# Float32 products between float16 ones: where the decay and a products, the scans and the weight splits of an RWKV-7 time mixer stand

## The chip, the cores and the metric

The kernel runs on one core of a Trainium2 chip. The metric is device time in microseconds (us) of one execution, the median of the runs shown. TensorE has two clock levels, 1.2 and 2.4 GHz; the profile gives the granted clock as a share of full speed (0.50 and 1.00).

## The reference, cut to what matters

Two layers of a streaming encoder over 528 positions (16 learned ones and 512) of 1024 channels. Each layer is a half-step SwiGLU FFN, a token mixer, another half-step FFN, each between RMSNorms. Layer 0's mixer is RWKV-7 with 16 heads of 64, layer 1's is attention in a window. The change touches RWKV-7 alone, ahead of its recurrence:

```python
xx = jnp.pad(h, ((0, 0), (1, 0), (0, 0)))[:, :-1] - h
xm = h[:, :, None, :] + xx[:, :, None, :] * mix          # r, k, v, w, a, g
rkv = jnp.einsum('blmc,mcd->blmd', xm[:, :, :3], w_rkv)
w_log = -jax.nn.softplus(-(w0 + jnp.tanh(xw @ w1) @ w2)) - 0.5
decay = jnp.exp(-jnp.exp(w_log))
a = jax.nn.sigmoid(a0 + (xa @ a1) @ a2)
g = jax.nn.sigmoid(xg @ g1) @ g2
kk = (k * k_k).reshape(B, L, H, N)
kk = kk / jnp.maximum(jnp.sqrt(jnp.sum(kk * kk, axis=-1, keepdims=True)), 1e-12)
k = k * (1 + (a - 1) * k_a)
```

Here w1 and a1 are 1024 x 64, w2 and a2 64 x 1024, g1 1024 x 160 and g2 160 x 1024.

## The kernel before, in words

Channels lie on partitions (8 tiles of 128), positions along the free axis. A large product in float32 quality is made of three float16 ones: weights and activations are each split into a high part and a rest, and high x high, high x rest and rest x high are summed in PSUM (`products`, line 287). A weight block comes by DMA into one of two halves of `stage`; ScalarE writes its high part (`split_hi`, line 256), VectorE its rest (`split_lo`, line 262). Every engine works through a program of its own in fixed order, with semaphores between them; the order is written out by hand in functions named after stage and engine.

The stages of RWKV-7 before the recurrence, in TensorE's order:

- **K**, then **V**: 8 tiles each (4 weight blocks `j` times 2 halves `s` of the positions); a tile is two groups ("halves") of 24 matmuls, one for each 128 output channels. A tile's two PSUM banks are copied out by VectorE (`evict`); three pairs of banks take turns (0 to 5), banks 6 and 7 are free for other use. During V ScalarE, VectorE and GpSimd make the mixtures for w and a: ScalarE scales the shifted input (`wa_prev`, line 942), VectorE adds (`wa_sum`, line 946), ScalarE makes the float16 high part (`wa_high`, line 951), GpSimd the rest (`wa_rest`, line 955), in four blocks `j`, each followed by one weight split.
- **The LoRA stage** (`lora_pe`, `lora_act`, `lora_dve`): first the products with w1 and a1 ("l products", `l_at`), into banks 6 and 7; tanh of the w part (`t_w`) on ScalarE, a copy of the a part (`t_a`) on VectorE. Then the gate's products with g1, four groups of 24 matmuls (`g_at`): two with 128 and two with 32 output channels. Meanwhile the mixtures for g and then for r are made; g's rests are VectorE's (line 955), and in the middle of them stands the split of R's second weight block, `r_jobs[1]`. Then the 16 products with w2 (decay, `w0` to `w7`) and a2 (`a0` to `a7`), line 1238: float32, 64 rows, two matmuls of 264 columns, four instructions each as the profile counts them. Each has two banks out of a ring of four pairs. ScalarE takes a sigmoid of each (line 1272), and VectorE a scan along time over each decay (line 1303).
- **R**: 8 tiles like V's. Between its halves stand the sums of squares over heads for kk (`sum_heads`, line 303, float32, 16 output rows; halves 1 to 4, two each) and the spreads of the inverse norms back to channels (`spread_heads`, line 311, float32, 16 rows in; halves 7 to 14, one each), all in banks 6 and 7. ScalarE makes the squares (line 1344), the root (line 1348) and the factors `f` (line 1353), VectorE the reciprocal (line 1383), and kk, k and b (`rates`, lines 1362 to 1368).
- **core**: the recurrence in chunks of 64, then the epilogue, which reads the gate and g2.

The semaphores of small steps are counters with names: `Steps.count(name)` is the place of the name in a list given once, and a wait for it waits until the counter has that value. It means "this step is done" only if steps are done in the order of the list. For `lo_act` the list is sg, sg2, tanh, w0 to w7, a0 to a7, where `sg` and `sg2` are the gate's two sigmoids (lines 1264 and 1266); ScalarE issues tanh (line 1256) first, then sg and sg2.

The activations' spill to DRAM (`s_spill`) frees the buffer `h` during these stages: it holds `sgate`, w2 and a2, `t_w`, `t_a` and r's scratch `tm_r`.

Of the kernel before, what the change touches and what calls it, by code (L numbers as in the profile page):

```python
# [22 lines left out]
ALU = mybir.AluOpType  # L23
# [74 lines left out]
def build(nc, xT, vecs, consts, w_gu, w_down, w_rkv, w_l1, w_g1, w_w2, w_a2, w_g2, w_out, w_q, w_k, w_v, b_v,  # L98
          w_o, rel_table, rel_hot, flip_rows, out):
    with ExitStack() as ctx:  # L100
# [742 lines left out]
        spreads = hflat[0:HEADS, 3104:3104 + D]  # L843
# [11 lines left out]
        def rwkv(T, T_out, ffn_before):  # L855
# [11 lines left out]
            lo_act = Steps(sem("lora_act"), ["sg", "sg2", "tanh"] + [f"{q}{k}" for q in "wa" for k in range(KT)])  # L867
# [11 lines left out]
            tm_r = hflat[:, 3104:4160].rearrange("p (s t) -> p s t", s=2)  # L879
# [201 lines left out]
            more = split_more[:, :]  # L1081
            dq = more[:, 0:2 * L].rearrange("p (u t) -> p u t", u=2)
            df = more[:, 2 * L:4 * L].rearrange("p (u t) -> p u t", u=2)
            norms = more[0:HEADS, 4 * L:5 * L]
# [3 lines left out]
            d_dve = Steps(sem("kk_dve"), ["spread", "max", "inv"] + [f"{q}{k}" for k in each for q in ("kk", "k", "b")])  # L1088
# [120 lines left out]
            seq = [(q, k) for q in "wa" for k in each]  # L1209
            rate_bank = [2 * ((g_at + 1) % 3), 6, 2 * ((g_at + 2) % 3), 2 * (g_at % 3)]  # L1210

            def lora_pe(e):
                e.wait_ge(w_lo, l_job.n + 1)
                e.wait_ge(wa_lo, 2 * KT)
                for s, q in enumerate("wa"):
# [5 lines left out]
                open_step(e, g_at, g_job)  # L1221
                for s, (c0, c1) in enumerate([(0, P), (P, 160)]):
# [5 lines left out]
                last.then_inc(done, 1)  # L1228
                e.wait_ge(s_w2, 32)
                e.wait_ge(lo_act.sem, lo_act.count("tanh"))  # L1230
                e.wait_ge(freed, l_at + 1)
                for z, (q, k) in enumerate(seq):
                    if z == 2:
                        e.wait_ge(freed, g_at + 1)
                    if z >= 4:
                        e.wait_ge(lo_act.sem, lo_act.count("%s%d" % seq[z - 4]))
                    for b, (a, m) in enumerate(ALL):
                        last = e.matmul(psum[:, rate_bank[z % 4] + b, 0:m],  # L1238
                                        (w2_sb if q == "w" else a2_sb)[:, k * P:(k + 1) * P],
                                        (t_w if q == "w" else t_a)[:, a:a + m], start=True, stop=True)  # L1240
                    last.then_inc(lo_pe.sem, lo_pe.step(f"{q}{k}"))

            def lora_act(e):
# [24 lines left out]
                e.wait_ge(padded.sem, padded.count("a"))  # L1268
                for z, (q, k) in enumerate(seq):
                    e.wait_ge(lo_pe.sem, lo_pe.count(f"{q}{k}"))  # L1270
                    dst = (c_all if q == "w" else a_all)[:, k, PAD:LP]
                    e.activation(halves(dst, n), psum[:, rate_bank[z % 4]:rate_bank[z % 4] + 2, 0:n],
                                 ACT.Sigmoid, bias=v("w0" if q == "w" else "a0", k)).then_inc(
                                     lo_act.sem, lo_act.step(f"{q}{k}"))

            def lora_dve(e):
                for k in range(4):
                    g_sum(e, k)
                for k in each:
                    g_rest(e, k)  # L1280
                    if k == 3:
                        split_lo(e, r_jobs[1])
# [17 lines left out]
                e.wait_ge(s_mask, 2)  # L1300
                for k in each:
                    e.wait_ge(lo_act.sem, lo_act.count(f"w{k}"))
                    e.tensor_tensor_scan(c_all[:, k], mask, c_all[:, k], 0.0, ALU.mult, ALU.add).then_inc(c_scan, 1)

            def gate_weights(e):

                e.wait_ge(lo_pe.sem, lo_pe.count(f"a{KT - 1}"))
                e.dma_start(g2_sb[:, 0], w_g2[0:P, :]).then_inc(s_g2, 16)
# [3 lines left out]
            def r_pe(e):  # L1312
                def sums(k0):
                    if k0 == 0:
                        e.wait_ge(lo_act.sem, lo_act.count("a5"))
                    for k in (k0, k0 + 1):
                        e.wait_ge(d_act.sem, d_act.count(f"sq{k}"))
                        sum_heads(e, 6, k, dq[:, k % 2]).then_inc(d_pe.sem, d_pe.step(f"sum{k}"))

                def inverses(k):  # L1320
                    if k == 0:
                        e.wait_ge(d_dve.sem, d_dve.count("inv"))
                    else:
                        e.wait_ge(d_dve.sem, d_dve.count(f"kk{k - 1}"))
                    spread_heads(e, 6, k, norms).then_inc(d_pe.sem, d_pe.step(f"inv{k}"))

                def after_tile(q):
                    if 1 <= q <= 4:
                        sums(2 * (q - 1))
                    elif 7 <= q <= 14:  # L1330
                        inverses(q - 7)

                for q, (j, s) in enumerate(in_order):
                    if q < 3:
                        e.wait_ge(lo_act.sem, lo_act.count(("a4", "a6", "a7")[q]))
                    tiles(e, r_at[j, s], r_jobs[j], x16, s,
                          (lambda k: e.wait_ge(r_lo, k + 1)) if q == 0 else None, None, lambda: after_tile(2 * q))
                    after_tile(2 * q + 1)

            def r_act(e):  # L1340
                for k in each:
                    if k >= 2:
                        e.wait_ge(d_pe.sem, d_pe.count(f"sum{k - 2}"))
                    e.activation(dq[:, k % 2], k_all[:, k, PAD:LP], ACT.Square, scale=v("k_k", k)).then_inc(
                        d_act.sem, d_act.step(f"sq{k}"))
                split_hi(e, r_jobs[2])
                e.wait_ge(d_pe.sem, d_pe.count(f"sum{KT - 1}"))
                e.activation(halves(norms, n), psum[0:HEADS, 6:8, 0:n], ACT.Sqrt).then_inc(
                    d_act.sem, d_act.step("root"))
                for k in each:  # L1350
                    if k >= 2:
                        e.wait_ge(d_dve.sem, d_dve.count(f"k{k - 2}"))
# [1326 lines left out]
```

## Time and profile before

| | us |
|---|---|
| median of 3 runs | 2321.61 |
| lowest and highest | 2320.35, 2323.71 |
| profiled execution | 2321.75 |
| its span | 2320.0 |
| TensorE busy in the span | 2228.7 (96%) |
| VectorE, ScalarE, GpSimd busy | 1075.0, 797.8, 500.7 |

The span is what the profiler's records cover; times of the trace count from its start. A row of the windows gives for a stretch how long each engine was busy, with the number of instructions, and TensorE's granted clock. A row of the instructions in order of time gives start, duration, engine, line, operation, operands and count, and in brackets how long the engine was idle before it and for whom. Matmul ends are modelled and overlap the next start; starts are better to count from.

### The profile page before, as it was taken

To read this page: it belongs to the slowest core of one execution; us is meant where nothing else is said; L and a number is where in the kernel's file an instruction comes from. 1 tells how busy PE (TensorE), PEld (TensorE's weight loads), DVE (VectorE), ACT (ScalarE), POOL (GpSimd) and SP (SyncE) were. 2 spreads that over 40 slices of the span, in tenths; PEclk is the share of its full clock that TensorE was granted. 3 is DMA by queue.
4 is the path that set the end of the run, shared out by engine and by line. 5 is a ranking of instruction groups with operands and counts; after the bars stand their busy time and mean duration, and the time that the engine had idled before them with its cause. 6 is when DMAs were issued, how large, how long until landed. Compare 5 with 4: busy or idle time off the path is not lost.

```text
span 2320.0 us, 50849 instructions
## 1 busy us (share of the span) xinstructions
PE 2228.7 (96%) x22812; PEld 1892.4 (82%) x22812; DVE 1075.0 (46%) x1455; ACT 797.8 (34%) x1356; POOL 500.7 (22%) x629
## 2 busy tenths in 40 slices
PE   7999999989899989899999999999999999999997
PEld 6888887877699965788888888888887668888886
DVE  5433326763566654553342273333274536533323
ACT  4333313664233331343332253333132434433320
POOL 2111114410132300531111241110153106211103
PEclk9999999997999995999999999999999779999998
DMA  4323311320000010323233123233214011232311
GB/s 157 128 97 118 125 62 55 122 73 12 2 4 4 4 41 21 142 96 110 92 119 116 41 89 113 92 113 117 80 55 118 1 37 70 100 105 101 141 51 37
DMA packets 28954, 183.42 MB, mean 79 GB/s; under 512 B 3217, under 2 KB 8145, under 8 KB 9793
## 3 DMA queue, kind: packets, MB, share of 16 engines
q1 hardware_dynamic: 27888, 178.79, 21.8%
q8 instruction: 180, 2.95, 0.5%
q0 software_dynamic: 848, 1.37, 0.3%
q14 instruction: 38, 0.30, 0.0%
HBM read 174.31 MB, written 4.30 MB: 77 GB/s over the span
## 4 chain that ended last, share of the span: by engine, by line
PE 87%; DVE 6%; POOL 3%; ACT 2%; issue 1%; DMA 0%; SPq 0%; POOLq 0%; ACTq 0%; DVEq 0%
PE psum L287 69%; PE psum L1561 5%; POOL h L347 1%; PE psum L1552 1%; PE psum L2338 1%; PE psum L2337 1%; PE psum L1894 1%; PE psum L1238 1%; PE psum L362 1%; PE psum L2324 1%; PE psum L311 1%; POOL x L398 1%; PE psum L1585 1%; PE psum L1896 1%; DVE split L262 1%
## 5 line engine op out<-in xcount | busy, mean ns | idle before, releaser
L287 PE MATMUL psum<-x,split 128*128 128x256 f16 (+1 forms) x5568 | 640.1, 277 | 10.5 <-POOL x L398 6.7
L287 PEld LDWEIGHTS psum<-x,split 128*128 128x128 f16 x5568 | 545.6, 98 | 102.1 <-issue 16.0
L287 PE MATMUL psum<-x,split_more 128*128 128x256 f16 (+1 forms) x2496 | 288.5, 277 | 1.5 <-DVE x L2436 1.5
L695 POOL TENSOR_TENSOR arena<-arena 128x256 f16<-128x256 f32 (+1 forms) x176 | 120.2, 683 | 771.3 <-ACT arena L544 771.3
L287 PE MATMUL psum<-x,arena 128*128 128x256 f16 (+2 forms) x2448 | 280.9, 276 | 0.3 <-POOL x L934 0.2
L287 PEld LDWEIGHTS psum<-x,split_more 128*128 128x128 f16 x2496 | 246.0, 99 | 38.5 <-issue 1.9
L287 PEld LDWEIGHTS psum<-x,arena 128*128 128x128 f16 (+1 forms) x2448 | 240.5, 98 | 35.0 <-POOL x L934 0.9
L262 DVE SCALAR_TENSOR_TENSOR split<-stage,split 128x2048 f16<-128x2048 f32 (+1 forms) x77 | 190.5, 2475 | 164.8 <-ACT split L256 164.8
L287 PE MATMUL psum<-arena,split 128*128 128x256 f16 (+1 forms) x2304 | 261.6, 276 | 0.0
L287 PEld LDWEIGHTS psum<-arena,split 128*128 128x128 f16 x2304 | 226.2, 98 | 33.3 <-issue 0.3
L622 DVE SCALAR_TENSOR_TENSOR arena<-psum,arena 128x256 f32<-128x256 f32 (+1 forms) x176 | 75.5, 429 | 320.8 <-ACT arena L538 316.3
L538 ACT ACTIVATE arena<-psum 128x256 f32<-128x256 f32 (+1 forms) x176 | 68.3, 388 | 384.3 <-PE psum L287 384.2
L256 ACT ACTIVATE split<-stage 128x2048 f16<-128x2048 f32 (+1 forms) x77 | 156.1, 2028 | 31.5 <-PE psum L287 29.7
L438 ACT ACTIVATE arena<-arena 128x272 f32<-128x272 f32 (+1 forms) x96 | 38.9, 418 | 360.0 <-DVE arena L425 336.9
L425 DVE TENSOR_SCALAR arena<-psum 128x272 f32<-128x272 f32 (+1 forms) x80 | 33.3, 428 | 249.6 <-PE psum L287 249.6
L287 PE MATMUL psum<-arena,split_more 128*128 128x256 f16 (+3 forms) x1248 | 144.1, 277 | 3.1 <-DVE arena L955 3.0
L287 PEld LDWEIGHTS psum<-arena,split_more 128*128 128x128 f16 (+1 forms) x1248 | 122.3, 98 | 23.0 <-DVE arena L955 4.3
L544 ACT ACTIVATE arena<-arena 128x256 f16<-128x256 f32 (+1 forms) x176 | 74.0, 421 | 185.9 <-DVE arena L627 185.9
L287 PE MATMUL psum<-arena 128*128 128x256 f16 (+2 forms) x1200 | 136.8, 275 | 0.0
L449 POOL TENSOR_TENSOR arena<-arena 128x272 f32<-128x272 f32 (+1 forms) x84 | 65.5, 780 | 324.7 <-ACT arena L438 321.5
L287 PEld LDWEIGHTS psum<-arena 128*128 128x128 f16 (+1 forms) x1200 | 117.8, 98 | 16.9 <-POOL arena L955 0.3
L262 DVE SCALAR_TENSOR_TENSOR split_more<-stage,split_more 128x2048 f16<-128x2048 f32 (+2 forms) x36 | 88.5, 2459 | 80.3 <-ACT split_more L256 80.3
(215 smaller groups left out, 2638.7 us busy)
## 6 DMA issues: line engine op xcount, KB each, us to landing
stage<-in_w_gu SPq DMA_DIRECT2D x88, 1024.0 KB, 4.9
stage<-in_w_down SPq DMA_DIRECT2D x32, 1408.0 KB, 6.0
stage<-in_w_rkv SPq DMA_DIRECT2D x12, 1024.0 KB, 4.9
stage<-in_w_out SPq DMA_DIRECT2D x4, 1024.0 KB, 4.9
stage<-in_w_q SPq DMA_DIRECT2D x4, 1024.0 KB, 4.7
stage<-in_w_o SPq DMA_DIRECT2D x4, 1024.0 KB, 6.2
h_spill<-h SPq DMA_DIRECT2D x1, 2112.0 KB, 11.6
h<-h_spill SPq DMA_DIRECT2D x1, 2112.0 KB, 11.1
```

The lines of the kernel that those rows point to most:

```text
L256: act.activation(job.split[:, 0, 0:job.cols], stage[:, job.u, 0:job.cols], ACT.Copy, scale=W_SCALE).then_inc(w_hi, 1)
L262: dve.scalar_tensor_tensor(out=job.split[:, 1, 0:job.cols], in0=stage[:, job.u, 0:job.cols], scalar=W_SCALE, in1=job.split[:, 0, 0:job.col ...
L287: last = pe.matmul(o, wt(wp, k), xs(xp, k), start=(k == 0 and wp == 0 and xp == 0), stop=(k == tiles - 1 and wp == 1))
L311: last = e.matmul(psum[:, b0 + b, 0:m], to, rows[:, a:a + m], start=True, stop=True)
L425: ins = dve.tensor_scalar(mix_out[:, m, a:a + n], bank(i, z)[:, 0:n], 1.0 / W_SCALE, None, ALU.mult)
L438: act.activation(osq[:, q % 2, 0:n], mix_out[:, m, a:a + n], ACT.Square).then_inc(out_sq, 1)
L449: pool.tensor_tensor(ssum[:, a:a + n], ssum[:, a:a + n], osq[:, q % 2, 0:n], ALU.add).then_inc(out_add, 1)
L538: e.activation(gate_s[:, no % 2, 0:n], bank(i)[:, 0:n], ACT.Sigmoid, scale=1.0 / W_SCALE).then_inc(gate_act, 1)
L544: e.activation(hid[s][:, 0, m, 0:n], hid32[:, no % 2, 0:n], ACT.Copy).then_inc(hid_hi, 1)
L622: e.scalar_tensor_tensor(out=gate_x[:, no % 2, 0:n], in0=bank(i)[:, 0:n], scalar=1.0 / W_SCALE ** 2, in1=gate_s[:, no % 2, 0:n], op0=ALU.m ...
L695: e.tensor_tensor(hid[s][:, 1, m, 0:n], hid32[:, no % 2, 0:n], hid[s][:, 0, m, 0:n], ALU.subtract).then_inc(hid_lo, 1)
L1561: last = e.matmul(o[p0:p0 + HD, q], a[p0:p0 + HD, 4 * f + q, 0:CH], b[p0:p0 + HD, 4 * f + q, 0:CH], start=(z == 0), stop=(z == len(terms) ...
```

## The change

The sums for kk move from R's halves 1 to 4 to V's halves 4 to 11 (one each), and the squares and the root with them; the squares' scratch `dq` and `norms` move into `h`, so the first square waits for the spill. The eight decay products go in pairs behind each of the gate's four groups, with two pairs of banks in place of four; tanh is now first in the list of `lo_act`. The a products go into R: one inside its first half, one after each of halves 0 to 6, all in banks 6 and 7. The eight scans, the reciprocal and the split of `r_jobs[1]` move into R on VectorE, the split's high part into R on ScalarE. The loads of g2 now wait for the last spread too. The spreads stay behind halves 7 to 14.

```diff
-            lo_act = Steps(sem("lora_act"), ["sg", "sg2", "tanh"] + [f"{q}{k}" for q in "wa" for k in range(KT)])
+            lo_act = Steps(sem("lora_act"), ["tanh"] + [f"w{k}" for k in range(KT)] + ["sg", "sg2"] + [f"a{k}" for k in range(KT)])
...
             def v_pe(e):
-                for j, s in in_order:
+                def sums(q):
+                    k = q - 4
+                    if 0 <= k < KT:
+                        e.wait_ge(d_act.sem, d_act.count(f"sq{k}"))
+                        sum_heads(e, 6, k, dq[:, k % 2]).then_inc(d_pe.sem, d_pe.step(f"sum{k}"))
+
+                for q, (j, s) in enumerate(in_order):
                     tiles(e, v_at[j, s], v_jobs[j], xa0, s,
-                          (lambda k: e.wait_ge(v_lo, k + 1)) if j == 0 and s == 0 else None)
+                          (lambda k: e.wait_ge(v_lo, k + 1)) if q == 0 else None, None, lambda: sums(2 * q))
+                    sums(2 * q + 1)
...
                     split_hi(e, v_after[j])
+                    if j == 0:
+                        e.wait_ge(s_spill, 16)
+                    for k in range(4 * j, 4 * j + 4):
+                        if k < KT:
+                            if k >= 2:
+                                e.wait_ge(d_pe.sem, d_pe.count(f"sum{k - 2}"))
+                            e.activation(dq[:, k % 2], k_all[:, k, PAD:LP], ACT.Square, scale=v("k_k", k)).then_inc(
+                                d_act.sem, d_act.step(f"sq{k}"))
+                e.wait_ge(d_pe.sem, d_pe.count(f"sum{KT - 1}"))
+                e.activation(halves(norms, n), psum[0:HEADS, 6:8, 0:n], ACT.Sqrt).then_inc(
+                    d_act.sem, d_act.step("root"))
...
-            rate_bank = [2 * ((g_at + 1) % 3), 6, 2 * ((g_at + 2) % 3), 2 * (g_at % 3)]
+            rate_bank = [2 * ((g_at + 1) % 3), 6]
...
             def lora_pe(e):
                 e.wait_ge(w_lo, l_job.n + 1)
                 e.wait_ge(wa_lo, 2 * KT)
+                e.wait_ge(d_act.sem, d_act.count("root"))
...
-                last.then_inc(done, 1)
-                e.wait_ge(s_w2, 32)
-                e.wait_ge(lo_act.sem, lo_act.count("tanh"))
-                e.wait_ge(freed, l_at + 1)
-                for z, (q, k) in enumerate(seq):
-                    if z == 2:
-                        e.wait_ge(freed, g_at + 1)
-                    if z >= 4:
-                        e.wait_ge(lo_act.sem, lo_act.count("%s%d" % seq[z - 4]))
...
+                        for u in range(2):
+                            if k == 0:
+                                e.wait_ge(s_w2, 32)
+                                e.wait_ge(lo_act.sem, lo_act.count("tanh"))
+                                e.wait_ge(freed, l_at + 1)
+                            if k >= 2:
+                                e.wait_ge(lo_act.sem, lo_act.count(f"w{k - 2}"))
+                            rate_product(e, "w", k, rate_bank[k % 2])
+                            k += 1
...
                 for k in each:
                     g_high(e, k)
-                    if k == 3:
-                        split_hi(e, r_jobs[1])
...
+                e.wait_ge(padded.sem, padded.count("c"))
                 for k in range(0, KT, 2):
                     for u in range(2):
                         r_prev(e, k + u)
                     for u in range(2):
                         r_high(e, k + u)
+                    for u in range(2):
+                        rate(e, "w", k + u, rate_bank[u])
...
                     g_rest(e, k)
-                    if k == 3:
-                        split_lo(e, r_jobs[1])
...
                 def after_tile(q):
+                    if q < KT - 1:
+                        e.wait_ge(lo_act.sem, lo_act.count(f"a{q}"))
+                        rate_product(e, "a", q + 1, 6)
+                    elif q < 2 * KT - 1:
+                        k = q - KT + 1
+                        if k == 0:
+                            e.wait_ge(lo_act.sem, lo_act.count("a7"))
+                            e.wait_ge(d_dve.sem, d_dve.count("spread"))
+                        else:
+                            e.wait_ge(d_dve.sem, d_dve.count(f"kk{k - 1}"))
+                        spread_heads(e, 6, k, norms).then_inc(d_pe.sem, d_pe.step(f"inv{k}"))
+
+                def first_rate(e, T, s):
+                    e.wait_ge(lo_act.sem, lo_act.count("w7"))
+                    rate_product(e, "a", 0, 6)
+
+                e.wait_ge(lo_act.sem, lo_act.count("w6"))
...
             def r_act(e):
+                e.wait_ge(padded.sem, padded.count("a"))
+                rate(e, "a", 0, 6)
+                split_hi(e, r_jobs[1])
+                for k in range(1, KT):
+                    rate(e, "a", k, 6)
+                    if k == 4:
+                        split_hi(e, r_jobs[2])
+                    if k < 3:
+                        factor(e, k - 1)
+                split_hi(e, r_jobs[3])
+                for k in range(2, KT):
+                    factor(e, k)
...
                 e.memset(r_all[:, :, 0:PAD], 0.0).then_inc(padded.sem, padded.step("r"))
+                split_lo(e, r_jobs[1])
+                e.wait_ge(d_act.sem, d_act.count("root"))
+                e.tensor_scalar(norms, norms, 1e-12, None, ALU.max).then_inc(d_dve.sem, d_dve.step("max"))
+                e.wait_ge(d_dve.sem, d_dve.count("max"))
+                e.reciprocal(norms, norms).then_inc(d_dve.sem, d_dve.step("inv"))
+                evict(e, r_at[0, 0], 0, 0, r_all)
                 e.wait_ge(r_lo, KT)
...
-                evict(e, r_at[0, 0], 0, 0, r_all)
+                e.wait_ge(s_mask, 2)
+                scan(0)
+                scan(1)
                 evict(e, r_at[0, 1], 0, 1, r_all)
+                scan(2)
+                scan(3)
                 split_lo(e, r_jobs[2])
...
                 evict(e, r_at[1, 0], 1, 0, r_all)
+                for k in range(4, KT):
+                    scan(k)
                 evict(e, r_at[1, 1], 1, 1, r_all)
```

`rate_product` is the two matmuls of one product, `rate` the wait for it with its sigmoid, `scan(k)` the wait for the sigmoid `w{k}` with its scan, `factor` the factor `f{k}`; the instructions are those of before.

## Rows read from the trace of the kernel before

**Rows 1.** The page: the span, and TensorE's granted clock in 40 slices of 58 us.
```profile
span 2320.0 us, 50849 instructions
...
PEclk9999999997999995999999999999999779999998
```

**Rows 2.** Windows by stretch: engines busy (x instructions), granted clock, DMA share, GB/s.
```profile
442.80:486.30 43.50, 43.49 (x387) 37.42 (x385) 26.39 (x30) 28.75 (x41) 22.58 (x20) 1.00 0.29 99
486.30:496.80 10.50, 10.50 (x98) 10.07 (x98) 9.53 (x12) 7.40 (x12) 0.00 (x0) 1.00 0.29 101
496.80:513.00 16.20, 13.05 (x97) 9.47 (x96) 15.55 (x22) 13.79 (x22) 0.00 (x0) 0.89 0.19 66
513.00:518.10 5.10, 0.07 (x2) 0.06 (x1) 3.22 (x6) 4.75 (x7) 0.00 (x0) 0.78 0.00 0
518.10:545.00 26.90, 26.90 (x65) 20.23 (x66) 11.78 (x10) 10.41 (x15) 0.00 (x0) 0.50 0.00 1
545.00:550.00 5.00, 5.00 (x23) 3.36 (x24) 0.00 (x0) 1.95 (x3) 0.00 (x0) 0.50 0.38 131
550.00:608.20 58.20, 58.20 (x427) 42.33 (x425) 29.01 (x35) 16.96 (x19) 0.00 (x0) 1.00 0.00 1
```

**Rows 3.** TensorE's instructions in order of time, gate's groups and the first products.
```profile
500.53 0.51 PE L287 MATMUL psum<-arena,split_more 128*128 128x264 f16 x3 [2.25 <-DVE arena L955]
501.83 11.21 PE L287 MATMUL psum<-arena,split_more 128*128 128x264 f16 x81 [0.79 <-DVE arena L955]
518.07 26.90 PE L1238 MATMUL psum<-h 64*128 64x264 f32 x64 [5.03 <-issue]
```

**Rows 4.** ScalarE's instructions in order of time: sigmoid's table, sg, sg2, w0's sigmoid.
```profile
515.59 1.28 ACT L1264 ACT_TABLE_LOAD   x1
516.88 0.61 ACT L1264 ACTIVATE h<-psum 128x528 f32<-128x528 f32 x1
517.39 0.58 ACT L1266 ACTIVATE h<-psum 32x528 f32<-32x528 f32 x1
520.26 0.70 ACT L1272 ACTIVATE arena<-psum,vec 128x528 f32<-128x528 f32 x1 [2.29 <-PE psum L1238]
```

**Rows 5.** TensorE's instructions in order of time, R: sums and a spread between halves.
```profile
557.66 1.95 PE L303 MATMUL psum<-split_more,cst 128*16 128x264 f32 x8
559.55 2.79 PE L287 MATMUL psum<-x,split 128*128 128x256 f16 x24
...
577.05 1.15 PE L311 MATMUL psum<-split_more,h 16*128 16x264 f32 x4
578.14 2.95 PE L287 MATMUL psum<-x,split 128*128 128x272 f16 x24
```

**Rows 6.** VectorE's instructions in order of time: first g sums, the split, t_a, a scan.
```profile
489.17 2.80 DVE L946 SCALAR_TENSOR_TENSOR arena<-arena,omm 128x528 f32<-128x528 f32 x4
...
496.88 2.29 DVE L262 SCALAR_TENSOR_TENSOR split<-stage,split 128x2048 f16<-128x2048 f32 x1 [0.81 <-ACT split L256]
...
503.04 0.71 DVE L1287 TENSOR_SCALAR h<-psum 64x528 f32<-64x528 f32 x1
...
521.07 1.36 DVE L1303 TENSOR_TENSOR_SCAN arena<-cumsum_buf,arena 128x576 f32<-128x576 f32 x1 [3.45 <-ACT arena L1272]
```

**Rows 7.** ScalarE's instructions in order of time: a split, four scaled copies, a square.
```profile
483.79 1.90 ACT L256 ACTIVATE split<-stage 128x2048 f16<-128x2048 f32 x1
485.64 2.62 ACT L942 ACTIVATE arena<-arena,vec 128x528 f32<-128x528 f32 x4
...
564.26 0.74 ACT L1344 ACTIVATE split_more<-arena,vec 128x528 f32<-128x528 f32 x1 [0.15 <-PE psum L303]
```

**Rows 8.** Windows of 2 us, epilogue and attention.
```profile
848.00:850.00 2.00, 1.42 (x8) 0.58 (x6) 1.87 (x3) 0.64 (x1) 0.00 (x0) 1.00 0.00 0
...
1836.00:1838.00 2.00, 2.00 (x10) 1.04 (x10) 0.00 (x0) 2.00 (x11) 0.00 (x0) 0.71 0.00 0
```

**Rows 9.** TensorE's instructions in order of time, attention: start of a float32 run.
```profile
1831.94 0.43 PE L2337 MATMUL psum<-arena 128*64 128x128 f32 x2
```

More of the change, by code:

```diff
@@ L842, in build @@
         sgate = hflat[:, 0:2 * L].rearrange("p (m t) -> p m t", m=2)
-        spreads = hflat[0:HEADS, 3104:3104 + D]
+        spreads = hflat[0:HEADS, 3168:3168 + D]
         w2_sb = hflat[0:HD, 1056:2080]
@@ L1087, in rwkv @@
             d_pe = Steps(sem("kk_pe"), [f"{q}{k}" for q in ("sum", "inv") for k in each])
-            d_dve = Steps(sem("kk_dve"), ["spread", "max", "inv"] + [f"{q}{k}" for k in each for q in ("kk", "k", "b")])
+            d_dve = Steps(sem("kk_dve"), ["max", "inv", "spread"] + [f"{q}{k}" for k in each for q in ("kk", "k", "b")])
             def early(e):
@@ L1206, in v_pool, with rate_product, rate @@
                 e.memset(starts[:, :, 0:1], 0.0).then_inc(s_mask, 1)
-            seq = [(q, k) for q in "wa" for k in each]
-            rate_bank = [2 * ((g_at + 1) % 3), 6, 2 * ((g_at + 2) % 3), 2 * (g_at % 3)]
+            rate_bank = [2 * ((g_at + 1) % 3), 6]
+            def rate_product(e, q, k, b0):
+                for b, (a, m) in enumerate(ALL):
+                    last = e.matmul(psum[:, b0 + b, 0:m], (w2_sb if q == "w" else a2_sb)[:, k * P:(k + 1) * P],
+                                    (t_w if q == "w" else t_a)[:, a:a + m], start=True, stop=True)
+                last.then_inc(lo_pe.sem, lo_pe.step(f"{q}{k}"))
+            def rate(e, q, k, b0):
+                e.wait_ge(lo_pe.sem, lo_pe.count(f"{q}{k}"))
+                dst = (c_all if q == "w" else a_all)[:, k, PAD:LP]
+                e.activation(halves(dst, n), psum[:, b0:b0 + 2, 0:n], ACT.Sigmoid,
+                             bias=v("w0" if q == "w" else "a0", k)).then_inc(lo_act.sem, lo_act.step(f"{q}{k}"))
             def lora_pe(e):
@@ L1221, in lora_pe @@
                 open_step(e, g_at, g_job)
+                k = 0
                 for s, (c0, c1) in enumerate([(0, P), (P, 160)]):
@@ L1227, in lora_pe @@
                                         (lambda k: e.wait_ge(g_lo, k + 1)) if s == b == 0 else None)
-                last.then_inc(done, 1)
-                e.wait_ge(s_w2, 32)
-                e.wait_ge(lo_act.sem, lo_act.count("tanh"))
-                e.wait_ge(freed, l_at + 1)
-                for z, (q, k) in enumerate(seq):
-                    if z == 2:
-                        e.wait_ge(freed, g_at + 1)
-                    if z >= 4:
-                        e.wait_ge(lo_act.sem, lo_act.count("%s%d" % seq[z - 4]))
[L1237 to L1241, printed above, removed]
+                        if s == b == 1:
+                            last.then_inc(done, 1)
+                        for u in range(2):
[7 more added lines that the diff above has]
+                            k += 1
             def lora_act(e):
@@ L1267, in lora_act @@
                              scale=1.0 / W_SCALE).then_inc(lo_act.sem, lo_act.step("sg2"))
[L1268 to L1274, printed above, removed]
             def lora_dve(e):
@@ L1299, in lora_dve @@
                 e.memset(eps[:, 2:3], 0.0).then_inc(freed, 1)
[L1300 to L1303, printed above, removed]
             def gate_weights(e):
                 e.wait_ge(lo_pe.sem, lo_pe.count(f"a{KT - 1}"))
+                e.wait_ge(d_pe.sem, d_pe.count(f"inv{KT - 1}"))
                 e.dma_start(g2_sb[:, 0], w_g2[0:P, :]).then_inc(s_g2, 16)
@@ L1312, in r_pe @@
             def r_pe(e):
[L1313 to L1325, printed above, removed]
@@ L1338, in r_pe @@
                     after_tile(2 * q + 1)
             def r_act(e):
[L1341 to L1349, printed above, removed]
@@ L1350, in r_act @@
-                for k in each:
-                    if k >= 2:
-                        e.wait_ge(d_dve.sem, d_dve.count(f"k{k - 2}"))
-                    e.activation(df[:, k % 2], a_all[:, k, PAD:LP], ACT.Identity, bias=ka1[:, k:k + 1],
-                                 scale=v("k_a", k)).then_inc(d_act.sem, d_act.step(f"f{k}"))
-                    if k == 1:
-                        split_hi(e, r_jobs[3])
+                e.wait_ge(padded.sem, padded.count("a"))
+                rate(e, "a", 0, 6)
@@ new lines, in r_act, with factor @@
+                split_hi(e, r_jobs[1])
[8 more added lines that the diff above has]
+                    factor(e, k)
+            def factor(e, k):
+                if k >= 2:
+                    e.wait_ge(d_dve.sem, d_dve.count(f"k{k - 2}"))
+                e.activation(df[:, k % 2], a_all[:, k, PAD:LP], ACT.Identity, bias=ka1[:, k:k + 1],
+                             scale=v("k_a", k)).then_inc(d_act.sem, d_act.step(f"f{k}"))
```

27 lines of the change are left out of this document (10 added, 17 removed).

## The prediction

> **What bounds the kernel now.** I read the page first, then a table of windows over the part of the time mixer that the change touches, then the instructions of each engine there in order of time. The page shows a TensorE that is busy nearly throughout, with one slice (522 to 580 us) where the granted clock sinks to 7 tenths [rows 1]. So TensorE sets the time, and a change can gain only where TensorE waits, or where it is busy at the lower of its two clocks. The table shows both [rows 2]. V (442.8 to 486.3) and R's later part (550.0 to 608.2) are full at clock 1.00 (2.4 GHz). In the gate's four groups (496.8 to 513.0) TensorE is idle 3.2 of 16.2 us. Then it stands 5.1 us. Then the 16 decay and a products fill 26.9 us at 0.50, which is 1.2 GHz, and R's first 5.0 us are at 0.50 too. The clock fell around 516, during the 5 us of standing, and the half-row float32 products that followed did not bring it back in 26.9 us of unbroken work. R's dense float16 did within 5 us.
>
> The 5.1 us are a count and no computation. The products wait for `lo_act.count("tanh")`; in the old list `tanh` is third, behind `sg` and `sg2`, but it is issued first. A count of three is reached only when the second gate sigmoid ends: it starts at 517.39 and takes 0.58, and the first product starts at 518.07 [rows 3, 4]. The profile calls this "issue".
>
> **The change, part by part.** All positions are on the profiled execution, 2321.75 us (its span and 1.75 around it); the median of the runs shown, 2321.61, is 0.14 below.
>
> *The wait for the gate's sigmoids* goes, since `tanh` is now first in the list: 5.0 us gained (5.03 by its row [rows 3]).
>
> *Products at the full clock.* A pair of sums over heads is eight instructions of the same 264 columns in float32 and takes 1.88 us at 1.00 (557.66 to the next tile half at 559.55), and one spread is four and takes 1.09 (577.05 to 578.14) [rows 5]. I take 1.98 for each of the four pairs of decay products (0.1 for returning to float16; bounds 1.8, below the pair shown, and 2.2, two spreads) and 1.05 for each a product by itself (bounds 0.94, half a pair, and 1.1): 4 x 1.98 + 8 x 1.05 = 16.3 us for what takes 26.9. Gain 10.6.
>
> *The gate's four groups.* The l products before them show 10.5 us for four such groups [rows 2]. The groups take 16.2, so 5.7 are waits and low clock: 2.25 + 0.79 for VectorE's rests, and a fall of the clock behind them [rows 3]. VectorE sets this: from 489.17 to 503.04 it makes sums and rests, with a weight split of 2.29 in the middle (496.88) and 0.8 of waiting for that split's other half [rows 6]. The split moves into R, so the chain is 13.9 - 3.1 = 10.8 us. Where does it begin? See V, next: 497.9, so it ends at 508.7, while TensorE reaches the first group at 505.4 and would end it at 508.0. The last rest holds it until 509.05: a wait of 1.0. VectorE's copy of `t_a` (0.7) follows and the first pair begins at 509.4: 0.35 more. Gain 5.7 - 1.35 = 4.3.
>
> *The sums into V.* TensorE's part: four pairs at 1.98 leave R, eight single ones at 1.05 enter V, 0.5 lost; V then lasts 43.5 + 8.4 = 51.9 us and ends near 494.9. ScalarE's part is where a stall could come from. A square is 0.74 us, and square k waits for sum k-2, so behind block j = 1 ScalarE stands until sum 5 (near 476), and blocks j = 2 and 3 of the w and a mixtures start 12 us later than before. A block is eight copies of about 0.66, 5.3 us [rows 7], some 6.5 with VectorE's answers. (0.74, 0.66 and the split's 1.90 are [rows 7] throughout.) Block 2 with its split ends near 484.5. Block 3's last sums stand behind VectorE's eviction of tile 6 (489.5), as now, so it ends near 492.2, the split of R's first weights (1.90) at 494.1, and the root, 0.6 and without a table load since V's last table was the Sqrt one, at 494.7. TensorE's new wait for `root` is thus met within 0.2 us of V's end; with a load of 1.28 [rows 4] it would be 1.1 late, which the wait for VectorE in the first group would then absorb. VectorE's split for R ends at 497.9, the start used above. Squares, root and spill are hidden; no gain from them leaving R, where TensorE was full.
>
> *New waits in the gate.* Product k waits for sigmoid k-2, and ScalarE puts two copies, two conversions and two sigmoids of 0.70 [rows 4] in one round: 1.3 + 1.3 + 1.4 = 4.0, against 2.62 + 1.98 = 4.6 for TensorE's round. The first round has also the pad (ScalarE now waits for it) and a table load: 509.4 + 0.7 + 1.3 + 1.4 + 1.3 + 0.7 = 514.8, where TensorE is ready at 514.0. Lost 0.8. The rounds after that are hidden. R's first tile uses the bank of product `w6`, whose sigmoid ends near 526.9; TensorE is ready at 526.0. Lost 0.9.
>
> By the Trainium skill ("ScalarE: Activation LUTs", What ACT_TABLE_LOAD costs) a switch of sets takes a drain of about 1.38 us on top of the 1.28 us load. Here the load at 515.59 is followed by its sigmoid at 516.88, with no such gap [rows 4]. By the page the two switches ahead of the first decay's sigmoid would cost 2.8 us more, and the time would be 2304.4.
>
> *R.* Its start was cold for 5.0 us, worth 2.5 [rows 2]; gained. On VectorE eight scans (1.36 each [rows 6]), the reciprocal and three splits now stand between evictions. Laid end to end at their present durations behind R's start, they give: tile 0's eviction near 538, needed at 550; the weights of tile 4 near 548, needed at 558; the scans done near 556, and the core needs them at R's end. Each is 10 us early, so R stays TensorE's; without that cover the 10.9 us of scans would push the evictions and R by as much as they are late. The two gate loads on the DMA queue leave later (after `inv7`, R's end); nothing is queued behind them that moves before the core has ended, and their reader is the epilogue, which comes after the core.
>
> **Sum.** 5.0 + 10.6 + 4.3 + 2.5 - 0.5 - 0.8 - 0.9 = 20.2 us. R would start near 526.9 instead of 545 and end near 588. 2321.75 - 20.2 = 2301.6.
>
> **The rivals.** (a) *The clock falls once*, where the last decay pair and the wait of 0.9 come together ahead of R, and R starts cold as it does now: 2.5 back, 2304.1. For it: a short stop follows low-row work. Against: sums and spreads between R's halves left it at 1.00 throughout. (b) *It falls after the gate's second group and stays low until R*: three pairs and two groups, 5.9 + 5.2, take twice as long, and R starts cold, 13.6 less the 0.9 wait that this covers: 2314.3. For it: in attention the clock fell around 1837 with TensorE never idle, in a run of float32 products of few rows or columns begun at 1831.94 [rows 9]; and the two last groups fill only 32 columns of the array. Against: in the epilogue float32 products with gaps held 1.00 (848 to 850) [rows 8], and those narrow groups held it before. The skill's rule ("TensorE: Matmul & The Clock Gate", What's actually happening) that activity releases the clock would exclude (b), but rows 2 show 26.9 busy us that released nothing, and the measurement decides. (c) *ScalarE is late in V*: I count 18 us from the last square to the end of the split for R, where today's last block waits for TensorE's tiles. If it takes 5 more, root comes near 500, TensorE stands 5 us at V's end, and the chain of rests, which then begins with root and not with the split, ends 3 us later than I have it: 2304.7. (d) *The wait of 5 us is not the count* and stays: 2306.6. (e) *Slower*: R's first half now has an a product in it, and every half one behind it. If such mixed work never lets the clock rise, (b) runs on into R. After (b)'s gate 20.2 + 0.9 - 11.1 = 10.0 of the gain are left. A half with its product is 2.7 + 1.05 at the full clock and costs as much again at the lower one, so from the third half on the kernel is slower than before, and after the eight halves with a products (30 us) it stands at 2301.6 + 10.2 + 30 = 2342. Against: R rose at 550 from cold by its float16, of which each half still has 2.7 us.
>
> **Chances.** Forecast 0.53, (a) 0.17, (b) 0.13, (c) 0.09, (d) 0.04, (e) 0.04. Range: with all new waits hidden and the low price for products, 2297; (b) is taken in, 2314.5. A measurement here tells about 0.2% (4.6 us) from no change. All cases but (e) are faster by more; with 0.02 for mixtures that end level: 0.94, 0.02, 0.04.
>
> **What would show it.** Right: no idle time over 1.5 us on TensorE from V to R's end; clock 1.00 throughout; a product pair at about 1.9 us where it was 3.5; R's end near 588. The first step fails if the first pair still starts after `sg2`; the second if the granted clock reads 0.50 between 510 and 530. The forecast is wrong above all if the clock's answer to half-row float32 products between narrow groups is not what sums between full tiles suggest.

## The result, and the profile after

The changed kernel takes 2306.62 us (median of 4 runs, 2305.11 to 2310.78), the kernel before beside it 2322.66: a ratio of 0.9935, 95% interval 0.992 to 0.9949. Measured a second time, it takes 2304.86 us against 2323.09, a ratio of 0.9918 (0.9904 to 0.9933). Both intervals lie below 1: the change makes the kernel faster by 0.7 to 0.8%. The forecast was 2301.6.

| us | before | after | after, again |
|---|---|---|---|
| profiled execution | 2321.75 | 2310.78 | 2302.27 |
| V's start to R's end | 165.4 | 145.8 | 145.8 |
| the rest of the span | 2154.6 | 2163.1 | 2154.6 |

The second line is what the change touches. It is read from the instructions in order of time: V begins at 442.8, 445.1 and 443.8, and R's last matmul ends at 608.2, 590.9 and 589.6. It lost 19.6 us, twice the same. The first profile of after is the longest of its four runs, and what hides its gain is the last line: 8.5 us more outside the stretch.

The page's clock line, after, in 40 slices of 58 us: the 7 of slice 10 in [rows 1] is a 9.

```profile
PEclk9999999999899986999999999999999769999999
```

Windows by stretch, after: V, the l products, the gate's groups with the decay products, R, and the stop behind R. They answer to [rows 2].

```profile
445.10:497.40 52.30, 52.30 (x418) 39.18 (x416) 29.45 (x30) 33.98 (x49) 24.33 (x20) 1.00 0.24 82
497.40:507.90 10.50, 10.50 (x98) 10.07 (x98) 10.26 (x14) 7.81 (x14) 0.00 (x0) 1.00 0.28 100
507.90:528.50 20.60, 19.74 (x129) 14.42 (x128) 15.56 (x24) 19.32 (x31) 0.00 (x0) 1.00 0.00 1
528.50:590.90 62.40, 62.36 (x448) 46.83 (x448) 42.65 (x48) 19.47 (x23) 0.00 (x0) 1.00 0.08 26
590.90:595.60 4.70, 0.05 (x1) 0.00 (x0) 3.78 (x8) 1.98 (x4) 0.00 (x0) 0.76 0.08 31
```

From V's start to R's end no window has a clock below 1.00. TensorE's instructions in order of time, after, from the gate's first group into R, answer to [rows 3]:

```profile
507.88 3.69 PE L287 MATMUL psum<-arena,split_more 128*128 128x264 f16 x24
511.90 2.02 PE L1231 MATMUL psum<-h 64*128 64x264 f32 x8 [0.32 <-DVE h L1307]
513.84 2.87 PE L287 MATMUL psum<-arena,split_more 128*128 128x264 f16 x24
516.65 2.04 PE L1231 MATMUL psum<-h 64*128 64x264 f32 x8
518.63 2.87 PE L287 MATMUL psum<-arena,split_more 128*32 128x264 f16 x24
...
526.21 2.04 PE L1231 MATMUL psum<-h 64*128 64x264 f32 x8
528.54 1.56 PE L287 MATMUL psum<-x,split 128*128 128x272 f16 x12 [0.29 <-ACT arena L1238]
...
536.59 1.15 PE L1231 MATMUL psum<-h 64*128 64x264 f32 x4
537.67 2.79 PE L287 MATMUL psum<-x,split 128*128 128x256 f16 x24
```

From start to start a pair of decay products takes 1.94 to 1.98 us (3.4 before: 26.9 over eight pairs), an a product 1.08; the idle times left in brackets are 0.32 and 0.29 us. ScalarE's instructions in order of time show the root without a table load before it, and the first decay sigmoid:

```profile
494.88 1.90 ACT L256 ACTIVATE split<-stage 128x2048 f16<-128x2048 f32 x1
496.68 0.58 ACT L1201 ACTIVATE h<-psum 16x528 f32<-16x528 f32 x1
...
514.61 1.28 ACT L1238 ACT_TABLE_LOAD   x1
515.90 1.29 ACT L1238 ACTIVATE arena<-psum,vec 128x528 f32<-128x528 f32 x2
```

### The profile page after: what moved, and what is told of

Same layout as the page of the kernel before. It is cut to its first block, busy times and chain, and to the rows that moved or that the text cites. A ratio compares the mean times of both kernels' runs of the same rounds, so it can differ in the third digit from the quotient of the medians.

```text
span 2308.9 us, 50850 instructions
## 1 busy us (share of the span) xinstructions
PE 2223.3 (96%) x22812; PEld 1883.0 (82%) x22812; DVE 1077.2 (47%) x1455; ACT 794.1 (34%) x1355; POOL 502.2 (22%) x629
## 4 chain that ended last, share of the span: by engine, by line
PE 87%; DVE 6%; POOL 3%; ACT 3%; issue 1%; DMA 0%; SPq 0%; POOLq 0%; ACTq 0%; DVEq 0%
PE psum L287 69%; PE psum L1589 6%; POOL h L347 1%; PE psum L1580 1%; PE psum L2366 1%; PE psum L2365 1%; PE psum L1922 1%; PE psum L362 1%; PE psum L2352 1%; PE psum L311 1%; PE psum L1613 1%; PE psum L1924 1%; PE psum L303 1%; DVE arena L339 1%; DVE split L262 1%
```

## The experiments

The theory to test: the clock fell because TensorE stood, and everything else of the gain is idle time. The rivals: the half-row float32 products lower the clock by themselves and float16 between them holds it (then the interleaving is what counts); mixed work cannot raise the clock; and, for the 4 us missing in the first medians, a loss in later stages that the change causes.

**Where the missing 4 us are.** The changed kernel as it is.

> The changed kernel once more, beside the kernel before. In the trace the stretch from V's first tile to R's end is 19.6 us shorter, while the medians differ by 16.0. Theory N (chance: the clock's falls outside the stretch lie differently from execution to execution, and the difference is not the change's): more rounds move the gain toward 19 us, and the profile's time outside the stretch differs from that of before by under 2 us. Theory S (the later stages lose some 4 us for a cause of the change): the gain stays near 16, and the same stage after R is longer again, by 2 us or more in the same place.

2304.86 us, ratio 0.9918 (0.9904 to 0.9933), 19.0 us by the ratio. The stretch is 145.8 us as in the first profile, and the rest of the span 2154.6, as in before to a tenth. So theory N holds. The first profile's extra 8.5 us are 1.3 ahead of V and 7.2 behind R, and its mean granted clock is 0.960 against 0.965, so the clock was low for longer there; which fall came from what was not followed one by one. The intervals of the two measurements overlap, and both are compatible with the 19.6 us of the traces or nearly so (2322.7 less 19.6 is a ratio of 0.9916).

**The count.** The kernel before with one list changed:

```diff
-            lo_act = Steps(sem("lora_act"), ["sg", "sg2", "tanh"] + [f"{q}{k}" for q in "wa" for k in range(KT)])
+            lo_act = Steps(sem("lora_act"), ["tanh", "sg", "sg2"] + [f"{q}{k}" for q in "wa" for k in range(KT)])
```

> The kernel before with tanh first in the list of names and nothing else. If the stop of 5 us is the count: TensorE begins products w0 and w1 near 513, 5 us earlier, at clock 1.00; the third waits for the gate's banks (sg2, near 518). Two products of 1.76 us leave the cold stretch: 3.5 us faster, 2318.5. If the shorter stop keeps the clock up, up to 15 us faster. If the stop is something else: 0, and the first product still at 518.

2321.09 us, ratio 0.9987 (0.9976 to 0.9999): 3 us faster by the ratio, and 3.9 in the trace's stretch from V's start to R's end (161.5 us for 165.4), where the count theory had 3.5. TensorE in order of time:

```profile
513.41 2.04 PE L1238 MATMUL psum<-h 64*128 64x264 f32 x8
519.08 23.35 PE L1238 MATMUL psum<-h 64*128 64x264 f32 x56 [3.62 <-DVE eps L1299]
542.36 7.73 PE L287 MATMUL psum<-x,split 128*128 128x272 f16 x48
```

The first two products start right behind the gate's groups and at the full clock. The rest wait 3.62 us for the banks of the gate's result. The granted clock still reads 1.00 in that stop (515.42 to 519.08) and 0.52 in the 4 us behind it, and 14 products run at 0.50. So the 5.03 us of "issue" were the count, and by itself its removal is worth only the two products that fit: one wait stood behind the other.

**What lowered the clock.** The kernel before, with float16 work in the stop and the products still in one block:

```diff
                 e.wait_ge(s_w2, 32)
-                e.wait_ge(lo_act.sem, lo_act.count("tanh"))
                 e.wait_ge(freed, l_at + 1)
+                for z in range(48):
+                    e.matmul(psum[:, rate_bank[0] + z % 2, 0:264], g_job.split[:, 0, 128:256],
+                             g_job.split[:, 0, 256:520], start=True, stop=True)
+                e.wait_ge(lo_act.sem, lo_act.count("tanh"))
```

> The kernel before with 48 float16 matmuls of 264 columns, whose result is not used, in the stop between the gate and the products, so that TensorE never stands there (the products stay in one block). Theory A (the stop lowered the clock; half-row float32 products in a row would hold it): the 16 products take 15 us instead of 26.9 and R starts warm, 14 us faster, 2308. Theory B (a row of such products lets the clock fall by itself, and what holds it in the changed kernel is float16 in between): the clock falls some us into the block, R starts cold, 1 to 4 us faster, 2319 to 2321.

2309.51 us, ratio 0.9941 (0.9926 to 0.9956): 13.6 us faster than before (15.1 in the stretch, 150.3 for 165.4), for 5.5 us of work that computes nothing. TensorE in order of time:

```profile
515.38 5.57 PE L1232 MATMUL psum<-split_more 128*128 128x264 f16 x48
520.88 13.72 PE L1241 MATMUL psum<-h 64*128 64x264 f32 x64
534.54 5.73 PE L287 MATMUL psum<-x,split 128*128 128x272 f16 x48
```

Two windows of it, the products and R's first part, in the columns of [rows 2]:

```profile
520.90:534.50 13.60, 13.60 (x65) 11.30 (x64) 11.01 (x10) 10.29 (x15) 0.00 (x0) 1.00 0.01 2
534.50:560.00 25.50, 25.50 (x188) 17.56 (x188) 6.86 (x5) 11.48 (x14) 0.00 (x0) 1.00 0.08 26
```

Theory A holds and B falls. The same 64 instructions that stayed at 0.50 for 26.9 us [rows 3] run 13.7 us unbroken at 1.00 when TensorE comes to them from work without a stop. These products kept the clock at either level that they found. The fill takes the stop away and puts dense float16 in its place; no run has the block with neither stop nor fill, so which of the two kept the clock at 1.00 is not told apart. In x1 and in the changed kernel the first pair runs at 1.00 right behind other work or a wait of 0.32 us, with no fill.

Interleaving is not needed to hold the clock in the gate. The changed kernel is another 4.6 us faster than this one (4.5 in the stretch, 145.8 for 150.3), but not because interleaved products are cheaper: they take 16.5 us, the block 13.7. What they save is the 5.5 us of fill, as sigmoids and products overlap with other work, and the move of the weight split saves 3.1 more (next experiment).

**The split's place.** The changed kernel with `split_hi` and `split_lo` of `r_jobs[1]` back in the gate's loops at `k == 3`.

> The changed kernel with the split of R's second weight block put back among the gate's rests on ScalarE and VectorE. If it was what made TensorE wait in the gate's first group: idle time there rises from 1.0 to about 4 us, and the clock falls behind it as before (1.7 us): 3 to 5 us slower than the changed kernel, 2310 to 2312. If the wait was only passed on, the same time as the changed kernel.

2309.23 us, ratio 0.9938 (0.9923 to 0.9953); by the medians 4.4 us slower than the changed kernel, and the stretch from V's start to R's end takes 148.9 us instead of 145.8. TensorE in order of time:

```profile
507.45 1.52 PE L287 MATMUL psum<-arena,split_more 128*128 128x264 f16 x12
511.20 0.81 PE L287 MATMUL psum<-arena,split_more 128*128 128x264 f16 x3 [2.22 <-DVE arena L955]
512.49 2.16 PE L287 MATMUL psum<-arena,split_more 128*128 128x264 f16 x9 [0.48 <-DVE arena L955]
```

The first wait is that of before (2.25). The second is shorter (0.48 for 0.79) only because the three matmuls ahead of it are longer (0.81 for 0.51). So the split in VectorE's and ScalarE's queues made these waits. The clock fell behind the first of them, and three windows show how long that lasted:

```profile
511.00:513.00 2.00, 1.32 (x6) 0.55 (x6) 2.00 (x5) 1.32 (x3) 0.00 (x0) 0.57 0.74 274
513.00:514.60 1.60, 1.60 (x9) 0.70 (x7) 1.43 (x4) 1.59 (x3) 0.00 (x0) 0.50 0.68 271
514.60:516.60 2.00, 2.00 (x10) 1.44 (x9) 1.95 (x4) 1.71 (x3) 0.00 (x0) 0.98 0.00 0
```

It was back for the first pair (2.00 us). While low it met little work, twelve matmuls, the last nine at some 240 ns each, and the stretch grew by 3.1 us, the lower end of the 3 to 5 expected.

**A stop in the middle of mixed work.** The changed kernel with a reciprocal of 16x768, its result unused, ahead of VectorE's copy of `t_a`:

```diff
+                e.reciprocal(cbuf[0:HEADS, 1, 0:8, :],
+                             c("ones")[0:HEADS, 0:96].unsqueeze(1).to_broadcast([HEADS, 8, 96]))
                 e.tensor_scalar(t_a.rearrange("p (s t) -> p s t", s=2), psum[HD:P, 6:8, 0:n],
```

> The changed kernel with a reciprocal of 16x768 (about 5 us, its result unused) on VectorE ahead of the copy of t_a, so that TensorE stands some 5 us before the first pair of decay products, as the kernel before did. Theory H (half-row float32 products hold either clock but do not raise it, and float16 between them does raise it): the clock falls during the stop, the first pair takes 3.5 us, and the second group or the next brings 1.00 back: 5 us of stop plus 2 to 4 of low clock, 7 to 9 us slower than the changed kernel, near 2313. Theory E (rivals b and e of the prediction: mixed work lets no clock rise): clock 0.50 until R at least, 5 + 14 us or more slower, 2324 and up.

2312.81 us, ratio 0.9954 (0.9939 to 0.9969): 8 us slower than the changed kernel in its second measurement. TensorE in order of time:

```profile
515.17 3.86 PE L1231 MATMUL psum<-h 64*128 64x264 f32 x8 [5.16 <-DVE h L1309]
518.96 5.01 PE L287 MATMUL psum<-arena,split_more 128*128 128x264 f16 x24
523.90 2.04 PE L1231 MATMUL psum<-h 64*128 64x264 f32 x8
525.87 2.88 PE L287 MATMUL psum<-arena,split_more 128*32 128x264 f16 x24
```

The theory called H in the expectation holds, and its 2313 is met to 0.2 us. The stop lowers the clock, the pair does not raise it (3.79 us), the one full float16 group behind it does, and from 524 to R's end the granted clock is 1.00, also through the narrow groups. Rival (e) of the prediction, that mixed work keeps a low clock low, falls for a mix with groups of 24 float16 matmuls of 128 output channels; whether the narrow groups alone would raise the clock was not run. Here interleaving does count: it limits the damage of a fall to 4 us (1.8 on the pair, 2.1 on the group), where the block and R's start lost 15.7 (13.2 and 2.5).

**Fills elsewhere.** The same theory says where else the kernel loses. `warm16` is a float16 view of constants; each matmul on it is 128 x 264 and goes into a bank about to be overwritten. Behind R's last tile:

```diff
                     after_tile(2 * q + 1)
+                e.wait_ge(freed, r_end - 1)
+                for z in range(40):
+                    e.matmul(psum[:, 2 * ((r_end - 2) % 3) + z % 2, 0:264], warm16[:, 0:128],
+                             warm16[:, 128:392], start=True, stop=True)
```

> The changed kernel with 40 float16 matmuls of 264 columns on constants (result unused) behind R's last tile, in the stop of 4.7 us before the recurrence. If a stop is what lowers the clock, the recurrence's first scores (5.9 us at 0.50) run at 1.00 in about 3: 2 to 5 us faster than the changed kernel, 2300 to 2303. If the low clock there has another cause, 0.

2303.62 us, ratio 0.9915 (0.99 to 0.9929): 1.2 us below the changed kernel, less than the 2 to 5 expected and than the width of either interval (7 us). The trace shows the effect: the core's first scores run 3.71 us instead of 5.83 to 5.90. Behind them comes a stop of 3.04 us for GpSimd, and 1.2 us after it the clock falls all the same:

```profile
595.84 3.71 PE L1586 MATMUL psum<-x 64*64 64x128 f32 x64 [0.19 <-DVE cumsum_buf L1812]
602.59 1.15 PE L1595 MATMUL psum<-split 64*64 64x64 f32 x32 [3.04 <-POOL split L1894]
```

```profile
602.50:603.70 1.20, 1.11 (x32) 1.04 (x32) 0.00 (x0) 0.38 (x1) 1.20 (x2) 1.00 0.00 0
603.70:606.00 2.30, 2.15 (x38) 1.92 (x38) 1.15 (x3) 0.90 (x2) 2.30 (x2) 0.54 0.00 0
```

In the epilogue, 36 matmuls in the 3.9 us in which TensorE waits for VectorE's reciprocal (`iv`):

> The changed kernel with 36 such matmuls in the epilogue, where TensorE stands 3.9 us for VectorE's reciprocal ahead of 50 us of float32 products at clock 0.50 (128, 32 and 16 rows). If unbroken float32 work holds a clock that it cannot raise, as x2_filled showed for 64 rows, the clock stays 1.00 and the 50 us shrink to 28 or more (VectorE's 2.9 us and its waits per channel tile bound a round from below): 15 to 22 us faster than the changed kernel, 2285 to 2290. If work of 16 and 32 rows lets it fall, as in attention: 0 to 5 us.

2300.61 us, ratio 0.9902 (0.9887 to 0.9917): 4 us faster than the changed kernel, not 15 to 22. TensorE in order of time, cut:

```profile
849.84 4.22 PE L1960 MATMUL psum<-cst 128*128 128x264 f16 x36
853.99 1.15 PE L311 MATMUL psum<-arena,h 16*128 16x264 f32 x4
...
857.00 0.83 PE L1924 MATMUL psum<-h 32*128 32x264 f32 x2
857.63 1.96 PE L311 MATMUL psum<-arena,h 16*128 16x264 f32 x4
```

The clock falls between 857 and 857.6, 3 to 3.6 us into products of 16, 128 and 32 rows and with no stop at all, and 41 us at 0.50 follow. So what x2 showed for 64 rows does not hold for this mix: part of theory B is true here. Which of the three shapes does it was not run; attention's run from 1831.94 to its fall near 1837 [rows 8, 9] alternates products of 128 and of 16 rows.

> Both fills together and 30 more matmuls between the recurrence's first scores and its first level, where TensorE stands 2.6 us: the sum of the two gains and up to 2 us more, 2280 to 2288 if both theories of the stop hold; near the changed kernel if neither does.

2297.68 us, ratio 0.9889 (0.9872 to 0.9905): both fills and one of 30 matmuls ahead of the first level add up (7 us on the changed kernel), and the expected 2280 to 2288 fails with the epilogue's part, for the reason x7 has.

**Float16 in between, where it is needed.** x8 with more such matmuls ahead of each of the seven later gate products:

```diff
+                    if k:
+                        for z in range(12):
+                            e.matmul(psum[:, (6 if k % 2 == 0 else 4) + z % 2, 0:264], warm16[:, 0:128],
+                                     warm16[:, 128:392], start=True, stop=True)
                     tot(6 if k % 2 == 0 else 4, g2_sb[:, 0, k * P:(k + 1) * P], sgate[:, 0],
```

> x8_fill_all with 12 more float16 matmuls of 264 columns (1.35 us, result unused) ahead of each of the seven later gate products of the epilogue. In x8 the clock fell 5 us into that float32 work of 128, 32 and 16 rows although TensorE was never idle, and a round took 6.47 us. If float16 in between holds the clock there, as R's sums and spreads suggest, a round takes 3.6 + 1.35 = 5.0 us: 7 x 1.5 = 10 us faster than x8, 2288. If the low-row work lets it fall all the same, each round takes 6.47 + 2.7: 19 us slower than x8, 2316.

2293.26 us, ratio 0.9867 (0.9852 to 0.9881), 2292.37 to 2293.53 in four runs: 4.4 us faster than x8, where 10 were expected (5.3 in the trace, from the first `spread_heads` of the epilogue to the next stage: 40.0 us for 45.2). Windows of 4 us over the epilogue:

```profile
858.00:862.00 4.00, 4.00 (x19) 2.84 (x18) 2.65 (x4) 0.38 (x1) 0.00 (x0) 0.67 0.00 0
862.00:866.00 4.00, 4.00 (x17) 2.12 (x16) 0.59 (x2) 0.27 (x1) 0.00 (x0) 0.90 0.01 4
866.00:870.00 4.00, 4.00 (x22) 2.58 (x19) 2.48 (x4) 0.64 (x1) 0.00 (x0) 1.00 0.00 0
...
878.00:882.00 4.00, 4.00 (x19) 2.75 (x19) 2.18 (x4) 0.03 (x1) 0.00 (x0) 0.73 0.00 0
882.00:886.00 4.00, 4.00 (x15) 2.14 (x14) 0.68 (x2) 0.64 (x1) 0.00 (x0) 0.84 0.00 0
```

The clock still falls in two of the seven rounds, but rises again each time. A round takes 4.71 to 4.81 us where it stays up and 6.34 where it falls, 36.3 for the seven, and 5.0 each, 35, were expected. Most of what was missing lies in x8: its seven rounds were taken at 6.47 each, 45.3, and take 40.7, since the clock falls only in the second of them (3.56 and 4.78, then five of 6.47). A round with the fill and the clock up is 1.15 us longer than one without (4.71 for 3.56).

> The same with 6 in place of 12 (0.67 us a round). If that is enough to hold the clock: rounds of 4.3 us, 15 us faster than x8, 2283. If it is too little: rounds of 6.47 + 1.35, 9 us slower, 2307. Between the two if it falls in some rounds only.

2302.23 us, ratio 0.9908 (0.9892 to 0.9925), 2297.9 to 2303.69. The profiled execution is the fastest of the four, as long as x8's (2298.04), so it can't stand for the median by itself; in its epilogue the clock falls in the third round and stays at 0.50 for the rest, so each round pays for its six matmuls at the low clock as well:

```profile
856.88 1.43 PE L1965 MATMUL psum<-cst 128*128 128x264 f16 x6
...
862.51 1.96 PE L311 MATMUL psum<-arena,h 16*128 16x264 f32 x4
864.40 1.50 PE L1965 MATMUL psum<-cst 128*128 128x264 f16 x6
```

The rows of the epilogue's first `spread_heads` and of the next stage's start, first x8's and then x10's:

```profile
851.71 1.15 PE L311 MATMUL psum<-arena,h 16*128 16x264 f32 x4
896.95 13.50 PE L287 MATMUL psum<-x,split 128*128 128x272 f16 x96 [2.60 <-DVE arena L2027]
...
847.72 1.15 PE L311 MATMUL psum<-arena,h 16*128 16x264 f32 x4
897.48 13.16 PE L287 MATMUL psum<-x,split 128*128 128x272 f16 x96 [2.60 <-DVE arena L2031]
```

From one to the other it is 45.2 us in x8 and 49.8 in x10. So half the fill made the epilogue 4.5 us longer than none; the medians differ by 4.6 in the same direction, but their intervals overlap. Where the first fall comes does not follow the amount of float16: it is 5.4 us behind the first of these rows in x8, 5.9 in x9 and 9.3 in x10, in one profile each. x9 is faster than both kernels, by 31 us than the one before and by 12 than the changed one in its second measurement (all of x5, x7 to x10 only add unused products).

## Why the prediction was right, point by point

The stretch lost 19.6 us where the sum said 20.2, and the time 2306.6, then 2304.9, lay 3 to 5 us above the 2301.6 forecast. Of that distance 0.6 us is in the stretch, and 0.9 to 1.3 lie in the starting point: the forecast counts from one execution of 2321.75, and the kernel before had medians of 2322.66 and 2323.09 beside the changed one. The other 3.5 and 1.4 us are scatter outside the stretch.

- *The wait for the sigmoids*, 5.0: gone. The first pair waits for `t_a` alone, and x1 shows the count as its cause. Rival (d) falls. But the prediction gives the whole 5.0 to the list, and x1 shows a second wait of 3.62 behind the first, for the banks of the gate's result; in the changed kernel it doesn't stand because the pairs use other banks.
- *Products at the full clock*, 10.6: four pairs at 1.97 and eight single ones at 1.08 are 16.5 us for 26.9, so 10.4. A pair before was 3.4 us, not the 3.5 that the prediction names at its end.
- *The gate's groups*, 4.3: the first pair starts 4.0 us after the l products' end; the forecast had 4.0 (509.4 less 505.4), 1.35 of it waiting. x3 confirms the split as the cause. The groups between pairs take 2.81 us, not 2.62, so a round is 4.78, not 4.60: 0.5 us undersized over three rounds. The prediction has 0.1 us for returning from float32 to float16 and puts it on the product pair; the group between two pairs is longer by 0.19 as well.
- *R's cold start*, 2.5: gained; 1.00 throughout.
- *The sums in V*, 0.5 lost: single ones take 1.00 each and V 52.3 us (51.9 forecast). The root ends at 497.3, 0.1 us before V, without a table load, as forecast. Rival (c) falls: ScalarE's blocks 2 and 3 followed at the pace assumed (block 3's split ends at 496.8, 2.7 us later than forecast, of which 2.3 are V's later start in this profile).
- *New waits in the gate*, 0.8 and 0.9 forecast as lost: oversized. The second pair starts at 516.65, within 0.1 us of the first sigmoid's end, with no idle time shown, and R's start waited 0.29. TensorE's longer rounds ate what the sigmoids needed.
- *R*: 61.2 us forecast, 62.4 measured, the mis-sized term again the return to float16 (sixteen insertions instead of twelve, and the first half is cut in two). Scans, reciprocal and splits cost nothing: tile 0 is evicted at 540.2, needed at 553.2 by tile 3's first half; the last scan ends at 558.
- *The drain that the Trainium skill adds to each switch of table sets* ("ScalarE: Activation LUTs", What ACT_TABLE_LOAD costs) doesn't show: the load at 514.61 starts right behind a conversion that ends at 514.6, and a sigmoid follows it at 515.90. The measurement decides for 1.28 us.
- *Rivals (a) and (b)*, 0.30 together: no profile of the changed kernel shows a fall in the stretch, and x2 says why. The reason given for the forecast (sums between R's halves left the clock up) was not the right one: 64-row products need nothing between them, at least for the 13.7 us of x2. That the forecast's clock came out was in this part luck. The reason given for (b) (attention's fall without a stop) is real for mixes that have products of 16 rows in them, as x7's epilogue shows again, and not for these 64-row ones.
- *(e)* falls with x4.

What the prediction left out is the scatter. It put the whole sum on one execution and gave the rest of the kernel no width; the rest differed by 8.5 us between two profiles of one kernel, and in x1 to x4, which leave it alone, it was 2156.1 to 2158.5.

## What to carry to other kernels

Read the granted clock next to the stops before them: work behind a stop can pay more for it than the stop's length, here 15.7 us (13.2 of the products, 2.5 of R) for 5.1 us of standing. Move or fill a stop ahead of sparse products first; interleave them with dense float16 so that a fall is short. Read behind the stop too: the fall can show only there (x1, x5). In a counter with named steps, put the names in the order in which they are issued, or a wait for the first is a wait for the last.

## What the runs showed of the hardware that was not expected

- Float32 products of 64 rows held whichever clock they found: 26.9 us at 0.50 after a stop of 5.1 us, 13.7 us at 1.00 after none.
- A mix of 16, 128 and 32 rows in float32 did not hold it: 1.00 was lost after 3 to 3.6 us of unbroken work (x7) and 5.2 us (x8, 851.7 to 856.9), behind 36 dense float16 matmuls in both.
- With 12 float16 matmuls a round (x9) the clock came back after each fall; with 6 (x10) it did not, in one profile of each.
- The clock could fall behind a stop and not in it: 1.00 through a stop of 3.62 us and 0.52 in the 4 us behind (x1), 1.00 through 3.04 us and 1.2 more (x5).
- The time outside the changed stretch was 2154.6 us before, and 2163.1 and 2154.6 in two profiled executions of the changed kernel.
